# Last feed-forward of a two-block kernel: every upward step from the fourth by seven products, weight sums of even steps on GpSimd, first convolution tap on ScalarE

## What is computed

```python
def conv_ffn(h, w_up, conv_w, conv_b, w_down):
    u = h @ w_up
    u = lax.conv_general_dilated(
        u, conv_w[:, None, :], window_strides=(1,), padding=[(CONV_W - 1, 0)],
        dimension_numbers=('NWC', 'WIO', 'NWC'), feature_group_count=2 * D_FF_2) + conv_b
    gate, val = jnp.split(u, 2, axis=-1)
    return (jax.nn.silu(gate) * val) @ w_down
...
x = x + conv_ffn(rms_norm_2(x, norm_ffn[l]), ffn_w_up[l], ffn_conv[l], ffn_conv_b[l], ffn_w_down[l])
...
return rms_norm_2(x, norm_final)
```

## Time and profile before

| | |
|---|---|
| median of 3 runs | 1778.19 us (1778.17 to 1778.53) |
| the profiled execution, its own time | 1778.32 us |
| its span | 1776.5 us, mean clock of TensorE 0.997 of full |
| busy, TensorE | 1716.2 us (97%) |
| busy, VectorE | 987.4 us (56%) |
| busy, ScalarE | 414.5 us (23%) |
| busy, GpSimd | 314.8 us (18%) |
| TensorE's share of the chain that ended last | 86% |

### The profile page before, as it was taken

The page is one execution under the profiler, slowest core; times in us unless marked ns, Lnnn a source line. Parts: engine busy times, 40 slices in busy tenths (PEclk is TensorE's granted clock), DMA queues, the critical chain, the costliest instruction groups (busy, mean ns, idle before and its releaser), DMA issues.

```text
span 1776.5 us, 27167 instructions
## 1 busy us (share of the span) xinstructions
PE 1716.2 (97%) x10938; PEld 1375.3 (77%) x10938; DVE 987.4 (56%) x1895; ACT 414.5 (23%) x803; POOL 314.8 (18%) x355
## 2 busy tenths in 40 slices
PE   7999999999999999999999999999999999999997
PEld 5434454488888888755799998877887788799997
DVE  1248652556676444496487764287831432288883
ACT  1312562222012110336322110323421101211110
POOL 0000271032001320006134110077000000001110
PEclk9999999999999999999999999999999999999999
DMA  7885324132242252320644445333222443344453
GB/s 284 321 310 192 142 93 149 68 143 95 95 143 97 93 189 76 138 95 26 235 167 167 167 166 190 119 130 134 95 73 78 161 142 119 118 146 164 166 170 116
DMA packets 38742, 256.32 MB, mean 144 GB/s; under 512 B 4160, under 2 KB 7360, under 8 KB 9056
## 3 DMA queue, kind: packets, MB, share of 16 engines
q1 hardware_dynamic: 34544, 228.29, 36.6%
q0 software_dynamic: 3504, 22.15, 3.2%
q10 hardware_dynamic: 576, 4.19, 0.6%
HBM read 247.28 MB, written 7.34 MB: 143 GB/s over the span
## 4 chain that ended last, share of the span: by engine, by line
PE 86%; DVE 8%; ACT 2%; POOL 1%; DMA 1%; issue 1%; ACTq 0%; DVEq 0%; SPq 0%; POOLq 0%
PE ps L683 85%; POOL aux L1956 1%; DMA ring<-weights 1%; PE ps L933 1%; DVE arena L2174 1%; DVE aux L2203 1%; DVE arena L2204 1%; DVE arena L2205 1%; DVE ring L2248 0%; DVE small L2216 0%; DVE aux L2105 0%; DVE aux L2109 0%; DVE aux L2106 0%; DVE aux L2110 0%; DVE aux L2107 0%
## 5 line engine op out<-in xcount | busy, mean ns | idle before, releaser
L683 PE MATMUL ps<-hT,ring 128*128 128x256 f32 (+3 forms) x3024 | 667.1, 381 | 6.5 <-ACT hT L1694 2.6
L683 PEld LDWEIGHTS ps<-hT,ring 128*128 128x128 f32 (+1 forms) x3024 | 515.0, 189 | 146.1 <-issue 86.1
L683 PE MATMUL ps<-arena,ring 128*128 128x256 f32 (+3 forms) x1884 | 355.5, 344 | 4.7 <-DVE arena L2205 3.4
L683 PEld LDWEIGHTS ps<-arena,ring 128*128 128x128 f32 (+1 forms) x1884 | 298.9, 191 | 50.5 <-issue 13.0
L683 PE MATMUL ps<-arena,sums 128*128 128x128 f32 (+1 forms) x966 | 161.6, 317 | 1.3 <-DVE aux L2274 1.3
L683 PEld LDWEIGHTS ps<-arena,sums 128*128 128x128 f32 x966 | 141.9, 191 | 12.1 <-DVE aux L2274 2.5
L1934 POOL TENSOR_TENSOR aux<-aux 128x256 f32<-128x256 f32 (+1 forms) x40 | 41.7, 1043 | 376.0 <-ACT aux L1499 307.3
L2247 DVE TENSOR_TENSOR sums<-ring 128x512 f32<-128x512 f32 x83 | 57.9, 697 | 64.4 <-PE ps L683 59.4
L683 PE MATMUL ps<-hT,sums 128*128 128x128 f32 (+1 forms) x592 | 89.3, 298 | 0.4 <-DVE aux L2274 0.4
L1956 POOL TENSOR_SCALAR aux<-aux,small 128x512 f32<-128x512 f32 (+1 forms) x48 | 70.9, 1487 | 79.7 <-DVE small L2223 79.1
L1977 POOL TENSOR_TENSOR arena<-arena 128x256 f32<-128x256 f32 (+1 forms) x32 | 26.5, 827 | 329.9 <-ACT arena L1688 329.9
(11 more groups left out here) (379 smaller groups left out, 1948.5 us busy)
## 6 DMA issues: line engine op xcount, KB each, us to landing
ring<-weights SPq DMA_DIRECT2D x212, 1024.0 KB, 4.9
arena<-ahead POOLq DMA_DIRECT2D x8, 1024.0 KB, 8.1
kept_turns<-aux ACTq DMA_DIRECT2D x4, 1024.0 KB, 5.7
arena<-kept_turns POOLq DMA_DIRECT2D x6, 512.0 KB, 6.4
kept_keys_values<-spare POOLq DMA_DIRECT2D x1, 2048.0 KB, 8.4
hT<-ahead POOLq DMA_DIRECT2D x2, 1024.0 KB, 6.1
spare<-ahead POOLq DMA_DIRECT2D x2, 1024.0 KB, 11.6
arena<-kept_keys_values POOLq DMA_DIRECT2D x1, 2048.0 KB, 8.5
```

The costliest lines, as they stand in the source:

```text
L683: ins = nc.tensor.matmul(o_, lhsT, rhs, start=start, stop=stop, skip_group_check=True)
```

## The change

- All steps from 3 to 21 go by seven products. Their chunks hold the same tiles in the order of the quads.
- The weight sums of the even ones (4, 6 ... 20) are made on GpSimd, by the same four operations (`weight_sums` in its list, semaphore `pool_sums`): those of step 4 before its loop, those of step 2kp+6 behind the hidden forms of pair kp. They wait for the chunk and for TensorE to leave the quad two before.
- ScalarE makes the first convolution tap of every tile (an Identity with scale and bias, semaphore `ftap`), VectorE the other two. ScalarE's two copies of the plain steps go.
- VectorE does the gate product of step i-1 ahead of the taps of step i, not behind them.

```diff
-UP_SEVEN = tuple(range(UP_RAW, FT2, 2))
+UP_SEVEN = tuple(range(UP_RAW, FT2))
+def on_pool(i):
+    return i in UP_SEVEN and i % 2 == 0
...
                         if i == 2 and j == 0:
-                            pe.wait_ge(S["quad_sums"], n_quad + 1)
+                            if what == "up" and on_pool(p):
+                                pe.wait_ge(S["pool_sums"], len([q for q in UP_SEVEN if q <= p and on_pool(q)]))
+                            else:
+                                given = len([q for q in UP_SEVEN if on_pool(q) and (what == "dn" or q < p)])
+                                pe.wait_ge(S["quad_sums"], n_quad + 1 - given)
...
                 if i in UP_SEVEN:
                     if i > UP_SEVEN[0]:
-                        taken(act, ("up", LAYERS, 0, i - 2, 1))
+                        taken(act, ("up", LAYERS, 0, i - 1, 1))
                     first_product(LAYERS, "up", 0, i)
-                elif UP_RAW <= i < FT2:
-                    for m in (2 * i, 2 * i + 1):
-                        copied(("up", m), fu[:, m % 8, 2:T + 2])
+                    taken(act, ("up", LAYERS, 0, i, 1))
+                if i < FT2:
+                    if i >= 2:
+                        act.wait_ge(S["fgate"], i - 1)
+                    for s_ in range(2):
+                        m, t_ = 2 * i + s_, s_ * FT2 + i
+                        if i < UP_RAW:
+                            taken(act, ("up", m))
+                        did(f(fc[:, m % 4, :], fu[:, m % 8, 2:T + 2], ACT.Identity, bias=col("ffn_conv_b_2", 0, t_),
+                              scale=col("ffn_conv_2", 0, 2 * 2 * FT2 + t_)), "ftap", wait=False)
...
+            def weight_sums(i):
+                n = quad_first[LAYERS, 0, "up", i, 0]
+                c, b = quad_chunk[n], n % 2
+                pool.wait_ge(landed[c % SLOTS], 16 * (c // SLOTS + 1))
+                pool.wait_ge(chunks_used, quad_chunk[n - 2] + 1)
+                a11, a12, a21, a22 = (ring[:, c % SLOTS, 4 * r:4 * r + 4, :].rearrange("p a b -> p (a b)") for r in range(4))
+                s2, s3, s4 = (sums[:, b, r, :] for r in range(3))
+                did(nc.gpsimd.tensor_tensor(s3, a11, a21, ALU.subtract))
+                did(nc.gpsimd.tensor_tensor(a21, a21, a22, ALU.add))
+                did(nc.gpsimd.tensor_tensor(s2, a21, a11, ALU.subtract))
+                did(nc.gpsimd.tensor_tensor(s4, a12, s2, ALU.subtract), "pool_sums", wait=False)
+            weight_sums(4)
             for kp in range(FT2 // 2):
                 pool.wait_ge(S["fgate"], 2 * kp + 2)
...
+                if on_pool(2 * kp + 6):
+                    weight_sums(2 * kp + 6)
...
             def conv_tile(m, i, s_):
-                did(ts(dst, u[:, 2:T + 2], col("ffn_conv_2", 0, 2 * 2 * FT2 + t_), col("ffn_conv_b_2", 0, t_), ALU.mult, ALU.add))
+                dve.wait_ge(S["ftap"], m + 1)
                 did(stt(dst, u[:, 1:T + 1], col("ffn_conv_2", 0, 2 * FT2 + t_), dst, ALU.mult, ALU.add))
                 did(stt(dst, u[:, 0:T], col("ffn_conv_2", 0, t_), dst, ALU.mult, ALU.add), "fconv")
...
                 if i < FT2:
-                    if i + 2 in UP_SEVEN:
+                    if i + 2 in UP_SEVEN and not on_pool(i + 2):
                         weight_sums(quad_first[LAYERS, 0, "up", i + 2, 0])
...
                 if i >= 1:
                     dve.wait_ge(S["fsilu"], i)
                     c = 2 * ((i - 1) % 2)
                     did(tt(fhid[:, i - 1, :], fc[:, c, :], fc[:, c + 1, :], ALU.mult), "fgate")
+                if i < FT2:
+                    for s_ in range(2):
+                        conv_tile(2 * i + s_, i, s_)
```

More of the change, by code:

```diff
@@ L578, in two_blocks @@
                   "s5_gelu", "y_s5_ready", "rw_shifted", "rw_squash", "rw_dve", "rw_act", "y_rw_ready", "merged", "h2_raw", "both",
-                  "pos_loaded", "x_square_sums", "ahead_norm2", "ahead_next", "ahead_last", "ahead_read", "square_sums", "rv_inverse", "h_half", "h_forms", "quad_sums", "first_product", "hid_forms", "x_next", "xmax", "xprob", "fconv", "fsilu", "fgate", "gains", "conv_first", "result", "h_scaled", "up_forms")
+                  "pool_sums", "ftap", "pos_loaded", "x_square_sums", "ahead_norm2", "ahead_next", "ahead_last", "ahead_read", "square_sums", "rv_inverse", "h_half", "h_forms", "quad_sums", "first_product", "hid_forms", "x_next", "xmax", "xprob", "fconv", "fsilu", "fgate", "gains", "conv_first", "result", "h_scaled", "up_forms")
         S = {n: sem(n) for n in names}
@@ L2669, in _ @@
                         weight_sums(down_first + i + 2 - FT2)
-                    for s_ in range(2):
-                        m = 2 * i + s_
-                        if i < UP_RAW:
+                    if i < UP_RAW:
+                        for m in (2 * i, 2 * i + 1):
                             finished(dve, ("up", m))
                             did(tt(fu[:, m % 8, 2:T + 2], bank(("up", m))[:, 0:T], rinv[:, xs], ALU.mult), key=("up", m))
-                        elif i not in UP_SEVEN:
-                            taken(dve, ("up", m))
-                        conv_tile(m, i, s_)
                 if i >= 1:
```

## The result

The changed kernel takes 1806.51 us (median of 4 runs, 1804.90 to 1807.69), the one before beside it 1778.36 us. The ratio is 1.0142, with a 95% interval of 1.0128 to 1.0157: slower by 23 to 28 us, where 41 were forecast. The lower reading, 1778.19 x 1.0142 = 1803.4 us, lies just under the range. The profiled execution took 1804.9 us with a span of 1803.1 and a mean clock of 0.993.

A forecast was written before the change was run, and what follows sets the result against it. VectorE was to become the bound, at 18.0 us per pair against 13.16: 34 us over seven pairs, +4.7 at the start and +2.8 for the last three steps, +41.3 on 1778.32, so 1819.5 us; range 1804 to 1830.

The forecast's parts named there:

- The bound and its place: In the last feed-forward's upward steps VectorE becomes the bound at 18.0 us per pair; TensorE waits 5 us for odd steps' sums.
- the signs: In the upward steps: VectorE near 100% busy, TensorE near 70%, a 0.7 us wait ahead of each combination.
- TensorE's 5.8 us: Nine plain upward steps become seven-product steps, 5.8 us less TensorE work, not seen because TensorE is no longer the bound.
- Hand-overs to ScalarE: VectorE waits in upward steps: 1.4 us per pair for Silu and copy, 0.2 for ScalarE's first tap, together 1.6.
- The price of a meeting: Each VectorE instruction with SBUF inputs that meets a 128x512 GpSimd addition loses 0.95 us; PSUM readers are spared.
- Which instructions meet: In each pair GpSimd's set meets VectorE's weight sums: three lose 0.95 us, the first 0.6, together 3.45 us.
- Hidden forms on taps: GpSimd's four 128x128 additions now fall beside four taps, at 0.14 us each, 0.6 us per pair.
- 9 us less: Lower end for taps: if GpSimd adds nothing to them, the whole loss is 9 us less, +32 instead of +41.
- the +2.8 of the last three steps: The last three upward steps have no GpSimd set but keep the hand-overs, costing +2.8 us.
- Half the collisions: Rival in the upward steps: only two of four additions have a partner, +28 us, 1806 us; chance 0.07.
- The late sums of GpSimd: Rival: TensorE waits on `pool_sums`; one microsecond over gives +7, 1826 us; chance 0.09 together with the dearer clock.
- The clock rival: TensorE's clock may halve after 5 us pauses, up to +12 us, 1831 us; chance 0.09 together with late sums.

## Why the prediction was right in kind and wrong in size

**The bound and its place: right.** VectorE became the bound, and TensorE waits for its last weight sum. Of the signs, VectorE's near 100% came; but TensorE is busy 148.6 of 169.7 us, 88% and not near 70%, and the wait ahead of each combination is absent.

**TensorE's 5.8 us: right,** 5.6 in the run without sums, and unseen in the changed kernel.

**The step that failed is the term "Hand-overs to ScalarE", 1.4 of its 1.6 us per pair.** The prediction, like the description of the change, said that the Silu waits for that step's taps, and that VectorE stands still for Silu and copy at the start of every step. The Silu works on the gate tile alone and its wait counts only that tile's taps: they are the first pair of the four. The taps of the value tile, 1.04 us, cover Silu and copy, 0.7 us. I had looked for cover ahead of the chain and found none; it lay inside. Moved to where the prediction had it, the wait costs 10.3 us (13.5 with no sets on GpSimd), most of the 15 between the forecast and the profile. The other 0.2 us, ScalarE's first tap, was right: 0.28 in even steps.

**The price of a meeting: right.** 0.95 us for a weight sum. For a tap, where no row decided, the upper end was taken, and taps are held indeed: 0.9 us for one beside a 128x512 addition.

**Which instructions meet: half right.** I said weight sums in every pair. They alternate: weight sums in one pair, taps in the next. Of the nine sets in the timelines five fell on weight sums, three on taps and one, the eighth, on some of each; they cost VectorE 2.8 to 3.9 us each, 29 in all. A pair takes 16 us, not 18, and GpSimd is released by TensorE, which is held only every second time; as I read the timelines, the set so starts later against VectorE in every other pair. It made little difference to the sum, as both pay about the same; that the walk which placed the sets had a wait in it that did not exist, and its sum still came out, is luck: 33 us of delays by the groups, hidden forms among them, and the prediction had 29.9 + 7 x 0.6 = 34. With the late Silu the same term is 5 us too high (24.7 for 29.9), since part of the set then falls beside PSUM readers; this is the other part of the distance to the forecast, 5 of the 15 us.

**Hidden forms on taps, 0.6 us per pair:** too high by the rows of the run without sums: the 44 taps that stand beside forms lost 3.3 us, 0.07 to 0.08 each and not 0.14. In the run without sets they cost 3.2 us. Two smaller figures do not come out of their terms: "9 us less" for the tap's lower end (its named terms make 7, so +34 and not +32), and the +2.8 of the last three steps (three half pairs at 12.4 + 1.6 + 0.6 against 13.16 make 2.2). Neither explains the distance.

**The rivals.** "Half the collisions" gives 1806 and hits the time, but not by its mechanism: not half but all of the collisions are there, and it is the hand-over that is missing. The late sums of GpSimd did not come: no wait on `pool_sums`. The clock rival: the lower clock did appear, in these windows of the changed kernel around the pause that ended at 1635.71:

```profile
1630.00:1635.70 5.70, 0.24 (x3) 0.05 (x1) 5.59 (x5) 1.03 (x2) 4.87 (x4) 0.84 0.43 167
1635.70:1638.70 3.00, 2.99 (x14) 2.99 (x15) 2.79 (x7) 0.58 (x2) 0.00 (x0) 0.50 0.00 0
1638.70:1641.70 3.00, 3.00 (x20) 3.00 (x20) 2.48 (x9) 1.09 (x2) 0.76 (x2) 0.66 0.00 0
1641.70:1644.70 3.00, 3.00 (x29) 3.00 (x29) 2.77 (x7) 0.58 (x2) 1.33 (x3) 1.00 0.33 41
```

After 5.5 us of standing, TensorE works at 0.50 and 0.66 of its clock (2.4 GHz falling to 1.2) for 6 us and loses (0.50 + 0.34) x 3 = 2.5 us. Behind the other three long pauses the same sum over 6 us gives 1.5, 1.7 and 2.4 us, so about 8 in all. The 32 us from one such pause to the next are filled by VectorE (29.6 busy and its gaps), which does not wait for TensorE in them. So the loss lies in TensorE's room. That is read from the profile; no run took the clock's drop away while keeping the pause. GpSimd's sets are released by TensorE, so a slower TensorE can also move what the next set meets; what that is worth no run shows.

## What to carry to other kernels

When VectorE is near its limit, look at what the work that moves to GpSimd reads: here, while both worked on tensors in SBUF, they took turns, and the work had in effect not been moved (+26.0 us with the sums on GpSimd, +21.4 with all on VectorE). Where VectorE had room, the place of the sums made no difference (-2.3 and -2.6). For a chain between two engines, look up which count each wait stands on, not which step: half a step's work behind the signal is cover for the other engine. And dose such a change: with its first tap on ScalarE, VectorE could carry the extra step in every second pair (-2.6 us), not in each (+21.4); without that relief even every second pair was too much (+10.0).

## What the runs showed of the hardware

- GpSimd's memsets of 128x1536, 1.38 us each, do not hold a VectorE tap with two tensors from SBUF (0.48 us); its additions of 128x512 do (1.37 to 1.55). Of VectorE's combinations, which read PSUM, none was held by them (0.29 us beside a set as elsewhere).
- The turns overlap a little: where they alternate in the changed kernel, one addition of each engine takes 1.67 us together (VectorE's starts 1630.68 and 1632.35), and the two alone would take 0.69 + 1.27 = 1.96.
- GpSimd is held as well, even by a trifle: in the run without forms its subtraction of one column took 0.19 us alone and 0.69 where a weight sum of VectorE was running:

```profile
1651.43 0.19 POOL L2048 TENSOR_TENSOR arena<-arena 128x1 f32<-128x1 f32 x1 [3.79 <-DVE arena L2704]
...
1702.16 0.69 DVE L2274 TENSOR_TENSOR sums<-ring 128x512 f32<-128x512 f32 x1
1702.20 0.69 POOL L2048 TENSOR_TENSOR arena<-arena 128x1 f32<-128x1 f32 x1 [9.95 <-DVE arena L2704]
```
